# Projection of the previous tile in two pieces instead of four, inside a chunked state-space scan

## The reference

```python
xdt = x * dt[..., None]
w = einsum('bcign,bcjgn->bcijg', cm, bm)[..., None] * decay
y = einsum('bcijgh,bcjghp->bcighp', w, xdt)                 # inside a tile
states = einsum('bcjgn,bcjghp->bcghpn', bm, xdt * decay_end[..., None])
h = h * chunk_decay + states                                # tile by tile
y = y + einsum('bcign,bcghpn->bcighp', cm, h_in) * exp(acs)[..., None]
y = (y + d_skip * xs) * silu(z_b)
y = rmsnorm(y per group, ssd_norm_w)                        # two groups
o_b = y @ w_o_ssd                                           # 1024 x 1024
merged = sigmoid(g_a) * o_a + sigmoid(g_b) * o_b
```

## Time and profile before

| | us |
|---|---|
| median of 3 runs | 2437.13 (2435.5 to 2437.49) |
| profiled execution, its own time | 2436.28 |
| its span in the trace | 2434.6 |
| TensorE busy in the span | 2288.5 (94%) |
| VectorE busy in the span | 812.7 (33%) |
| granted TensorE clock, mean | 0.968 of full speed |

### The profile page before, as it was taken

The page is one execution under the profiler, slowest core; times in us unless marked ns, Lnnn a source line. Parts: engine busy times, 40 slices in busy tenths (PEclk is TensorE's granted clock), DMA queues, the critical chain, the costliest instruction groups (busy, mean ns, idle before and its releaser), DMA issues. The chain is left out here.

```text
span 2434.6 us, 35230 instructions
## 1 busy us (share of the span) xinstructions
PE 2288.5 (94%) x12671; PEld 2062.2 (85%) x12671; DVE 812.7 (33%) x1504; ACT 831.1 (34%) x1925; POOL 636.8 (26%) x547
## 2 busy tenths in 40 slices
PE   6999999999999999999999679999946999996999
PEld 5999999999999999999999668888734878874887
DVE  4211100014444100100000065555517999973221
ACT  5211111124444211221111165555525666742010
POOL 3101011011011011010110055555517767760000
PEclk9999999999999999999999879999976999997999
DMA  4411121111121111211112964444345777735333
GB/s 165 89 72 54 71 71 71 71 70 71 64 77 71 71 70 62 88 54 71 70 71 82 67 165 109 106 120 120 87 118 147 188 195 197 203 104 173 130 129 99
DMA packets 281028, 250.09 MB, mean 103 GB/s; under 512 B 75209, under 2 KB 258361, under 8 KB 273785
## 3 DMA queue, kind: packets, MB, share of 16 engines
q1 hardware_dynamic: 278856, 248.79, 35.8%
q10 hardware_dynamic: 2112, 0.53, 0.1%
HBM read 158.48 MB, written 90.81 MB: 102 GB/s over the span
## 5 line engine op out<-in xcount | busy, mean ns | idle before, releaser
L74 PE MATMUL acc<-h_hi,w_hi 128*128 128x424 f32 (+1 forms) x2280 | 810.5, 355 | 10.2 <-DVE h_lo L561 7.8
L75 PE MATMUL acc<-h_lo,w_hi 128*128 128x424 f32 (+1 forms) x2280 | 807.3, 354 | 0.0
L76 PE MATMUL acc<-h_hi,w_lo 128*128 128x424 f32 (+1 forms) x2280 | 807.0, 354 | 0.0
L74 PEld LDWEIGHTS acc<-h_hi,w_hi 128*128 128x128 f32 x2280 | 430.2, 189 | 24.7 <-DVE h_lo L561 8.6
L332 POOL TENSOR_TENSOR w_lo<-w_raw,w_hi 128x1024 fp32r<-128x1024 f32 x57 | 144.7, 2539 | 1130.5 <-ACT w_hi L374 1130.5
L75 PEld LDWEIGHTS acc<-h_lo,w_hi 128*128 128x128 f32 x2280 | 430.6, 189 | 7.3
L76 PEld LDWEIGHTS acc<-h_hi,w_lo 128*128 128x128 f32 x2280 | 430.2, 189 | 7.3
L399 ACT ACTIVATE row<-acc 128x424 f32<-128x424 f32 (+1 forms) x215 | 112.7, 524 | 825.5 <-PE acc L76 825.4
L597 DVE SCALAR_TENSOR_TENSOR conv_acc<-conv_in,conv_wb,conv_acc 128x424 f32<-128x424 f32 (+2 forms) x216 | 126.1, 585 | 380.9 <-ACT conv_acc L444 373.1
L1120 ACT ACTIVATE a_prob<-a_score,a_neg_max 128x129 f32<-128x129 f32 x264 | 103.3, 398 | 45.9 <-DVE a_neg_max L1259 43.1
L74 PE MATMUL a_o_ps<-a_w_hi,a_at_hi 128*128 128x512 f32 (+1 forms) x272 | 117.0, 430 | 2.0 <-DVE a_branch L1292 2.0
(11 more groups left out here) (218 smaller groups left out, 3045.0 us busy)
## 6 DMA issues: line engine op xcount, KB each, us to landing
proj<-row SPq DMA_DIRECT2D x56, 1056.0 KB, 4.0
w_raw<-in_w_in_dram SPq DMA_DIRECT2D x28, 1024.0 KB, 5.2
s_feat<-proj SPq DMA_DIRECT2D x16, 1280.0 KB, 8.6
s_acs_b<-acs_dram SPq DMA_DIRECT2D x16, 1024.0 KB, 7.5
a_q_diag<-proj SPq DMA_DIRECT2D x66, 128.0 KB, 4.4
a_z<-proj SPq DMA_DIRECT2D x16, 512.0 KB, 4.7
a_gate_t<-proj SPq DMA_DIRECT2D x16, 512.0 KB, 4.6
branch_rows<-a_branch SPq DMA_DIRECT2D x16, 512.0 KB, 3.2
```

Of the source, the lines that this page charges most:

```text
L74: pe.matmul(out, hi, whi, start=first, stop=False)
L75: pe.matmul(out, hi, wlo, start=False, stop=False)
L76: return pe.matmul(out, lo, whi, start=False, stop=last)
```

## The change

TensorE's step had its four projection pieces apart: one behind the core of group 0, one between the two `x_rows`, and two around the gates. Now the two pieces of half 0 stand behind the core of group 0, and the two pieces of half 1 behind the core of group 1, `products` and the first `x_rows`; the second `x_rows` is the last thing in the step. On VectorE `merge(m - 1, 0)` moves ahead of `skipped(m, 1)`, and the second `times_dt` moves behind the second `mixed` and `square_sums`. Nothing is added or removed.

```diff
@@ VectorE, step(m, slot) @@
                 inter(m, slot, 1)
                 update(m, 1)
+                if has_prev(m):
+                    merge(m - 1, 1 - slot, 0)
                 skipped(m, slot, 1)
                 if has_next(m):
                     times_dt(m + 1, 1 - slot, 0)
                     masked(m + 1, 1 - slot)
                     mixed(m + 1, 1 - slot, 0)
-                if has_prev(m):
-                    merge(m - 1, 1 - slot, 0)
+                    mixed(m + 1, 1 - slot, 1)
+                square_sums(m)
                 if has_next(m):
                     times_dt(m + 1, 1 - slot, 1)
-                    mixed(m + 1, 1 - slot, 1)
-                square_sums(m)
@@ TensorE, step(m, slot) @@
                 core(m, slot, 0)
                 prev(gates, 0)
                 prev(run, 0, 0)
+                prev(run, 0, 1)
                 if has_prev(m):
                     squares(m - 1)
                 core(m, slot, 1)
                 if has_next(m):
                     products(m + 1, 1 - slot)
-                if has_next(m):
                     x_rows(m + 1, 1 - slot, 0)
-                prev(run, 0, 1)
+                prev(run, 1, 0)
+                prev(run, 1, 1)
+                prev(gates, 1)
                 if has_next(m):
                     x_rows(m + 1, 1 - slot, 1)
-                prev(run, 1, 0)
-                prev(gates, 1)
-                prev(run, 1, 1)
```

## The result

The changed kernel took 2524.24 us (median of 4 runs, 2520.84 to 2527.02), the kernel before 2437.31 beside it (4 runs, 2435.5 to 2437.77): 1.0355 times as long, 95% interval [1.0339, 1.0372]. Slower by 87 us, as forecast in sign; the forecast of 2501 was 23 us short, and its range, 2460 to 2526, held the time near its upper end. The profiled execution took 2522.64, its span 2520.9.

A forecast was written before the change was run, and what follows sets the result against it. TensorE was taken as the bound, VectorE close behind; a new loop of 3.36 + 18.60 + 1.2 = 23.16 us a step replaces 20.18, giving 2478 with the clock kept, plus 22.5 for half clock: 2501 us, range 2460 to 2526.

The forecast's parts named there:

- The ring: Loop of merge, piece (0, 1), squares, core of group 1, VectorE's remaining step, next merge: 23.16 us a step with clock kept.
- VectorE's way: From the core of group 1 to the end of L1994 in the next step, mostly VectorE: 18.60 us.
- the half clock: TensorE idles 3.3 us ahead of run(m-1, 0, 1), then 3 us at half clock: 1.5 us a step, 22.5 in all.
- merge, piece, squares, without clock: TensorE, from the merge to the core of group 1: 0.15, piece 2.85, squares 0.36, together 3.36 us.
- POOL's wait: VectorE's update waits for POOL's to_ends and decay behind the late second times_dt: 1.2 us a step.
- behind step 16, one piece less: Behind the core of step 16 TensorE runs one piece less than before, saving 2.85 us.
- rival 2: Half clock lasts longer, 6.3 us behind each gap, losing 3.2 us a step: 2526 us, chance 0.13.
- The short form for the first gate product: L1998, gate multiplication of half 0 on VectorE, taken short because POOL is waiting for skipped there: 0.32 us off.
- Rival 1: The wait is there but the clock stays up in nearly all steps: 2478 us, chance 0.24.
- Covered as said: Step 1: the moved piece falls into TensorE's 8.37 us wait for update, so the core of group 1 stays at 1870.51.
- its cover: first_part(m-1, 0) ends some 1.9 us behind the core, before merge(m-1, 0) at 3.86; losing this costs up to 1.4 a step.
- Rival 3: Not slower: the merge is in time and the new piece starts without a gap: 2429 us, chance 0.05.

The follow-up runs named there:

- the piece alone: Kernel before, with only run(m-1, 0, 1) moved directly behind run(m-1, 0, 0), ahead of squares; VectorE's order unchanged: 2467.25 us, ratio 1.0125.
- TensorE's moves alone: Kernel before, with the changed kernel's order on TensorE and the old order on VectorE: 2542.42 us, ratio 1.0431.
- the filled gap: Changed kernel, with the matmuls of run(m-1, 0, 0) done twice, 12 more a step: 2494.27 us, ratio 1.0227.
- `times_dt` back: Changed kernel, with VectorE's second times_dt put back ahead of the second mixed: 2510.53 us, ratio 1.0293.
- VectorE's moves alone: Kernel before, with the changed kernel's order on VectorE and the old order on TensorE: 2508.74 us, ratio 1.0293.
- the merge first: Changed kernel, with merge(m-2, 1) moved from behind skipped(m, 0) to the start of VectorE's step: 2458.48 us, ratio 1.0082.

## Why the prediction was right, and what it mis-sized

**The ring** was named rightly and all its signs came: busy share 84% (expected some 85), the gap ahead of the piece 3.85 to 3.99 (expected 3 to 4), VectorE idle ahead of L2004, POOL's L1721 releasing L1963 after a wait of 1.01, PEclk below 1.00. The experiments show it rather than argue it: the piece alone makes a ring of 22.37, and opening it at the merge brings the step to 20.58. The step of 26.1 is longer than the expected 23 to 25. What was mis-sized are two terms of the sum, VectorE's way and the half clock.

The profiled execution, 2522.64, against 2501:

| term | forecast | measured | difference, whole scan |
|---|---|---|---|
| merge, piece, squares, without clock | 3.36 | 3.36 (0.15 + 2.85 + 0.36) | 0 |
| VectorE's way with POOL's wait | 18.60 + 1.2 | 2105.99 - 2085.32 = 20.67 | 13 x 0.87 = 11.3 |
| half clock, a step | 1.5 | 26.09 - 24.03 = 2.06; 2.4 in step 2 | 13 x 0.56 + 0.9 = 8.2 |
| step 16 | 24.66 | 23.00 | -1.7 |
| behind step 16, one piece less | 2.85 | 12.36 - 10.53 = 1.83 | +1 |
| ahead of the first moved instruction | 0 | 3.8 | +3.8 |
| VectorE's new order in step 0 | 0 | 0.6 | +0.6 |

These make 23.2 us; the stages behind the scan took 1.4 less in this execution, which leaves 21.8 for the 2522.64 - 2501 = 21.6. The 3.8 us ahead of every moved instruction are no effect that this argument explains: in the traces of the other kernels the scan begins 1.8 to 6.7 us later than in that of the kernel before as well. With the first two terms right, the forecast would have been some 2520. And rival 2's number, 2526, is nearer to the measured 2524.24 than the forecast; that is a coincidence, since its half clock of 3.2 us a step did not come.

**VectorE's way, the first mis-sized term.** I took its instructions at the durations they had in the old order. Now the two `mixed` stand together, and POOL's `low` runs beside them from 2094.22 on:

```profile
2093.39 4.16 DVE L1932 TENSOR_TENSOR s_mix<-s_mix,s_gm 128x1024 f32<-128x1024 f32 x2
2097.47 1.75 DVE L1970 TENSOR_TENSOR s_work<-s_work 128x512 f32<-128x512 f32 x1
```

From start to start the pair takes 2097.47 - 2093.39 = 4.08. Before it took 3.50:

```profile
2082.73 1.95 DVE L1932 TENSOR_TENSOR s_mix<-s_mix,s_gm 128x1024 f32<-128x1024 f32 x1
2084.60 0.73 DVE L1994 SCALAR_TENSOR_TENSOR s_rows<-s_o_ps,s_stat,s_rows 128x512 f32<-128x512 f32 x1
...
2086.90 1.71 DVE L1932 TENSOR_TENSOR s_mix<-s_mix,s_gm 128x1024 f32<-128x1024 f32 x1
2088.53 1.77 DVE L1970 TENSOR_TENSOR s_work<-s_work 128x512 f32<-128x512 f32 x1
```

(1.87 + 1.63.) `square_sums` went from 2.87 to 3.11 and `masked` to `mixed` from 0.94 to 1.17; POOL's wait was 1.01 and not 1.2. Together 0.58 + 0.24 + 0.23 - 0.19 = 0.86. That POOL's work beside it is the cause is not shown, since no run took `low` away. Two things speak for it. The same instruction took 1.22 us at 2109.13 in the kernel with TensorE's moves alone, where POOL stood idle until 2109.39; as the second of the two it took 1.71 in the kernel before, with `low` beside it for 0.62 us, and 2.29 in the changed kernel, with `low` beside it from end to end. And `low` itself went from 3.97 to 4.46 us:

```profile
2094.22 4.46 POOL L1738 TENSOR_TENSOR s_y_lo<-s_work,s_y_hi 128x512 fp32r<-128x512 f32 x2
```

The short form for the first gate product was right: L1998 behind the merge (0) took 0.69.

**The half clock, the second.** The mechanism was right, and the filled gap shows it alone. I took the loss as half of 3 us. The piece took 4.82 on the mean of 13 steps, 1.97 above 2.85, and in a third of the steps `squares` and the start of the core are still slow, 0.3 more: 1.97 + 0.1 = 2.1. The filled kernel gives the same 2.1. Rival 1, that the clock stays up, fell: it went down in all 14 steps.

**Covered as said:** in step 1 the piece fell into the gap of 8.37, which is now 5.33. From there to the core of step 2 the changed kernel took 1903.16 - 1874.90 = 28.26, of which 2.4 is clock: 25.86, against 1896.4 - 1870.5 = 25.9 forecast. `first_part` kept its cover in the changed kernel. At the end one piece less saves 1.83 and not 2.85, since `gates` there then waits 0.78 for ACT.

Rival 3, not slower, rested on the lead of the merge in the steady step; the piece alone shows that the lead is eaten up, as argued.

## What to carry to other kernels

Before a wait is moved forward on one engine, follow the ring through what the other engine does between that wait's releaser and its own next wait; its length is a floor for the step, and it can be summed from the old trace to a few per cent (22.4 against 22.37, and 23.16 against 24.0). Then look at how much idle time the ring leaves TensorE in one piece: gaps of 3.9 us cost about 2 us more behind each, gaps of 2.2 us 1.5 in most steps, and filling those of 3.9 paid 30 us in all. And orders of two engines are made for each other: the halves of a move on both can each be worse, or hardly better, than the whole.

## What the runs showed that I had not expected

- **More matmuls, less time.** 12 additional matmuls a step (2.8 us of work) made the changed kernel 30 us faster, 2494.27 against 2524.24.
- **The clock fell behind shorter gaps than I had rows for, and stayed up behind some longer ones.** In the scans of all eleven kernels, gaps of 0.24 to 1.75 us ahead of a piece were followed by pieces of 2.80 to 3.03. Gaps of 3.85 to 3.99 (changed kernel) and of 3.25 to 3.29 (`times_dt` back) cost the clock in all 14 steps, those of 3.21 to 3.32 with VectorE's moves alone in 11 of 15. The kernel with TensorE's moves alone has gaps of 2.1 to 2.2 ahead of the piece (0, 1), each with one of 2.4 12 to 14 us ahead: in 12 of its 14 steps the piece took 4.3 to 4.4, in two 2.85. In the kernel with the merge first, one of 2.41 cost nothing and one of 2.93 did. The gap's length alone does not decide it between 2.1 and 3.3 us, and what else does is not shown. Windows of it behind a gap of 2.37, behind one of 2.23, and behind one of 2.21 that cost nothing:

```profile
2103.00:2106.00 3.00, 3.00 (x9) 2.35 (x10) 0.79 (x1) 0.00 (x0) 3.00 (x3) 0.59 0.72 175
2117.00:2120.00 3.00, 3.00 (x9) 2.28 (x9) 0.86 (x1) 2.04 (x4) 0.31 (x1) 0.53 0.00 0
2090.30:2093.00 2.70, 2.70 (x12) 2.23 (x13) 1.07 (x1) 2.38 (x4) 0.52 (x1) 1.00 0.00 0
```

  The Trainium skill, in "TensorE: Matmul & The Clock Gate", section "Why this matters for your kernels", asks for no idle gaps above about 3 us. Here 2.2 us was already too much in most steps, while 3.2 to 3.3 left the clock up in 4 of 15; the measurement decides, and I would keep gaps under 1.4.
- **A load behind a waiting store.** One load issued behind a store that waits for its data cost 12 us in one kernel (2458.48 against 2446.58) and 4 us in the kernel before (2437.15 against 2432.87), with the bytes unchanged.
